# Gathering the experts head by head, with the query projection and the key transposes in the same stage

## The reference

```python
q = einsum('td,de->te', xb, w_q)          # 8 heads x 2 halves x 128
s = einsum('thpd,hpkd->thpk', q, keys)    # 128 scores for each token, head and half
s_top, i_top = lax.top_k(s, 16)
cand = s_top[:, :, 0, :, None] + s_top[:, :, 1, None, :]       # 256 sums for each head
best, sel = lax.top_k(cand, 16)
eidx = (i_top half 0) * 128 + (i_top half 1), taken at sel     # 16 experts for each token and head
gate = softmax(best)
act  = gelu(einsum('td,thkd->thk', xb, u_tab[eidx]))
out  = einsum('thk,thkd->td', gate * act, v_tab[eidx])
```

## Time and profile before

| | us |
|---|---|
| median of 3 runs | 2713.84 (2705.30 to 2722.43) |
| profiled execution | 2712.25 |
| its span | 2710.5 |
| start of the phase `queries` | 1019.67 |
| first gather issued | 1185.48 |
| last gather issued | 2689.80 |

### The profile page before, as it was taken

The page is one execution under the profiler, slowest core; times in us unless marked ns, Lnnn a source line. Parts: engine busy times, 40 slices in busy tenths (PEclk is TensorE's granted clock), DMA queues, the critical chain, the costliest instruction groups (busy, mean ns, idle before and its releaser), DMA issues.

```text
span 2710.5 us, 24179 instructions
## 1 busy us (share of the span) xinstructions
PE 1893.6 (70%) x8692; PEld 1256.1 (46%) x8692; DVE 1364.3 (50%) x2693; ACT 524.8 (19%) x1028; POOL 1161.3 (43%) x1083
## 2 busy tenths in 40 slices
PE   4988696788776878704766676666667575757577
PEld 4987696487646778701323232222223232323232
DVE  2253543511564432386555655656565646564652
ACT  4223121022103242201112111121111121112111
POOL 0010110100011010037677767677767777777774
PEclk9997798699868888957888888787878787878789
DMA  3221111141224304149999999999999999999997
GB/s 113 81 64 47 32 40 44 44 138 42 90 92 149 106 11 124 32 164 325 360 370 367 384 354 365 369 357 375 374 373 350 375 349 385 347 362 362 375 362 282
DMA packets 237486, 632.51 MB, mean 233 GB/s; under 512 B 20655, under 2 KB 97791, under 8 KB 236994
## 3 DMA queue, kind: packets, MB, share of 16 engines
q0 software_dynamic: 149760, 545.33, 53.4%
q1 hardware_dynamic: 87626, 85.92, 10.0%
HBM read 615.46 MB, written 15.80 MB: 233 GB/s over the span
## 4 chain that ended last, share of the span: by engine, by line
issue 56%; PE 2%; DMA 1%; POOL 0%; SPq 0%; DVE 0%; ACT 0%
PE ps L1668 2%; POOL ex_u_row L1621 0%; DMA ex_v_row<-in_peer_v,ex_eidx 0%; DMA ex_gate_s<-again_gate 0%; SPq L1602 0%; DMA again_x<-x_ffn 0%; DVE h_tok L1827 0%; DVE h_tok L1821 0%; ACT ex_junk_a L1705 0%; SPq L1608 0%; ACT ex_ms L1707 0%; SPq L1606 0%; SPq L1605 0%; DVE ex_ms L1826 0%
## 5 line engine op out<-in xcount | busy, mean ns | idle before, releaser
L1668 PE MATMUL ps<-ex_v_row,ex_spread 128*128 128x512 f32 (+1 forms) x2080 | 974.1, 632 | 548.2 <-DMA ex_v_row<-in_peer_v,ex_eidx 495.3
L1668 PEld LDWEIGHTS ps<-ex_v_row,ex_spread 128*128 128x128 f32 (+1 forms) x2080 | 417.2, 202 | 1103.8 <-issue 585.7
L1808 DVE CUSTOM_DVE_ANT_0 ex_u_row<-ex_u_row,x_ffn 128x1024 f32<-128x1024 f32 x512 | 626.8, 1226 | 256.9 <-DMA ex_u_row<-in_peer_u,ex_eidx 224.8
L1621 POOL DMA_INDIRECT ex_u_row<-in_peer_u,ex_eidx x512 | 529.3, 1034 | 328.2 <-DVE ex_gate L1801 168.2
L1621 POOL DMA_INDIRECT ex_v_row<-in_peer_v,ex_eidx x512 | 519.9, 1015 | 270.9 <-issue 158.3
L1699 ACT ACTIVATE ex_spread<-square,ex_coef 128x128 f32<-128x128 f32 (+1 forms) x520 | 204.3, 399 | 1238.5 <-issue 583.8
L1815 DVE TENSOR_TENSOR ex_coef<-ex_coef,ex_gate 128x16 f32<-128x16 f32 x32 | 5.6, 176 | 276.3 <-ACT ex_coef L1692 200.4
L533 PE MATMUL ps<-proj_b_whi,x_lo 128*128 128x256 f32 (+1 forms) x320 | 90.7, 283 | 9.2 <-DVE proj_b_wlo L474 9.2
L582 POOL TENSOR_TENSOR dp_w_lo<-dp_w_raw,dp_w_hi 128x1024 fp32r<-128x1024 f32 x8 | 19.2, 2407 | 167.6 <-ACT dp_w_hi L608 167.6
L326 POOL TENSOR_TENSOR x_ffn<-norm_xn,norm_gains_row 128x1024 f32<-128x1024 f32 (+1 forms) x5 | 14.0, 2810 | 179.1 <-ACT norm_xn L281 179.1
L535 PE MATMUL ps<-proj_b_whi,x_hi 128*128 128x256 f32 (+1 forms) x320 | 90.4, 282 | 0.0
(11 more groups left out here) (392 smaller groups left out, 3504.1 us busy)
## 6 DMA issues: line engine op xcount, KB each, us to landing
ex_u_row<-in_peer_u,ex_eidx POOLq DMA_INDIRECT x512
ex_v_row<-in_peer_v,ex_eidx POOLq DMA_INDIRECT x512
proj_a_raw<-in_w_in SPq DMA_DIRECT2D x7, 1024.0 KB, 4.9
proj_b_raw<-in_w_in SPq DMA_DIRECT2D x7, 1024.0 KB, 5.3
queries_raw<-in_peer_wq SPq DMA_DIRECT2D x7, 1024.0 KB, 5.8
dp_w_raw<-in_w_in SPq DMA_DIRECT2D x8, 512.0 KB, 4.0
S_sample<-in_state_ret SPq DMA_DIRECT2D x1, 4096.0 KB
out_ret_s<-S_sample SPq DMA_DIRECT2D x4, 1024.0 KB, 4.5
```

The costliest lines, as they stand in the source:

```text
L1621: pool.indirect_dma_start(row[n % RING][:, :], None, table, bass.IndirectOffsetOnAxis(ap=where, axis=0)).then_inc(done[n % RING], 16)
L1668: ins = pe.matmul(k.pv[t % 2][0:r, c, :], spread[:, n % RING, 0:r], v_row[n % RING][:, c * 512:(c + 1) * 512], start=(i == 0), stop=(i == ...
L1808: dve.tensor_tensor_reduce(u, u, x, 1.0, 0.0, ALU.mult, ALU.add, coef[:, n:n + 1]).then_inc(dotted, 1)
```

## The change

- The phases `queries` and `turn_keys` are gone. Their work is inside `experts`, for one half head (128 columns, 512 KB of weights) at a time: `upper` on ScalarE, `lower` on VectorE, `queries` on TensorE, and a copy of the product on ScalarE. The keys and the first two blocks of weights are loaded during `norm2`.
- The unit of the retrieval is a head of a tile (32 units and 8 more for the sample tokens). `retrieve(u)` does for one head what the 8 parts did for eight, in fewer instructions or on fewer columns, and reads the scores from PSUM.
- VectorE's order: four `lower`, `retrieve(0)`, two `lower`, `retrieve(1)`, two `lower`, and then for each unit its 16 dots, the retrieval of the unit two ahead, and `weigh`. In units 0, 1 and 2 the last eight `lower` lie between dots. In units 20 to 27 a retrieval of a sample head follows the other one.
- GpSimd issues only gathers of u in units 0, 1 and 2 (`LEAD` = 3). From unit 3 on gathers of u and v take turns one by one, v three units behind; in units 10 and 18 two gathers of v go with each of u, after which v is two units behind, then one.
- `RING` is 7. The residual goes to DRAM during `norm2` (2 MB) and comes back tile by tile to `fin`. The softmax has its exponent and its sum in one ScalarE instruction for each head, with `Exp` and `Gelu` in turns.

The diff, cut to its core; the removed bodies of `turn_keys` and `experts` stand above:

```diff
--- before.py
+++ after.py
...
-GROUP = 16
 PER_ROW = HK * NS // P
-RING = 8
+RING = 7
...
+                for tiles, dst, s in stores:
+                    sp.wait_ge(summed, tiles)
+                    sp.dma_start(dst, s).then_inc(stored, 16)
+                wait(sp, stored, 16 * (len(extra) + len(stores)))
...
+def experts(k, a, o, x_hi, x_lo, x_ffn, h_store, again, early):
...
+    UNITS = TILES * PH
+    SAMPLE = UNITS
...
+    LEAD, BOTH = 3, (10, 18)
+    sums, w = {}, 0
+    for u in range(LEAD, UNITS + 1):
+        sums[u] = range(w, w + 1 + (u in BOTH))
+        w = sums[u].stop
+    summed_in = {w: u for u in sums for w in sums[u]}
+    turns = [0, 1]
+    after = {}
+    for u in range(UNITS):
+        after[u] = [u + 2] * (u + 2 < UNITS) + [SAMPLE + u - 20] * (20 <= u < 20 + PH)
+        turns += after[u]
+    place = {u: j for j, u in enumerate(turns)}
+    known = {u: 2 + sum(len(after[x]) for x in range(u + 1)) for u in range(UNITS)}
...
+        q, keysT = sb("q", [P, HP, T]), sb("keysT", [P, HP, NK])
...
+        x_rep, gain = (w[:, :, :].rearrange("p c n -> p (c n)") for w in w_raw)
+        coef, spread = sb("coef", [P, SLOTS]), sb("spread", [P, RING, P])
+        fin, ms = sb("fin", [P, 2, D]), sb("ms", [P, NT])
...
+        def slots(u):
+            return range(TOPK * u, TOPK * u + (TOPK if u < SAMPLE else PER_ROW))
...
+        def score_bank(j):
+            return k.pb[6 + j % 2][:, 0:2 * NK]
...
+                def fetch(t):
+                    r = ROWS[t]
+                    wait(sp, stored[t % 2], 16 * (t // 2))
+                    sp.dma_start(fin[0:r, t % 2, :], h_store[t * P:t * P + r, :]).then_inc(h_loaded[t % 2], 16)
+                def result(t):
+                    out = o["y_p"][0, t * P:(t + 1) * P, :] if t < TILES else o["y_s"][:, 0, :]
+                    sp.wait_ge(ready, t + 1)
+                    sp.dma_start(out, fin[0:ROWS[t], t % 2, :]).then_inc(stored[t % 2], 16)
+                    if t + 2 < NT:
+                        fetch(t + 2)
...
+                for n in range(2, HP):
+                    sp.wait_ge(split, n - 1)
+                    sp.dma_start(w_raw[n % 2][:, :, :], columns(a["peer_wq"][0], n * P, P)).then_inc(w_loaded[n % 2], 16)
...
+                fetch(0)
+                fetch(1)
+                result(0)
+                result(1)
...
             @block.gpsimd
             def _(pool):
...
+                def up(u, n):
+                    t, h = tile_head(u)
...
+                    wait(pool, dotted, n - RING + 1)
+                    pool.indirect_dma_start(u_row[:, n % RING, :], None, a["peer_u"][0],
+                                            bass.IndirectOffsetOnAxis(ap=where, axis=0)).then_inc(u_loaded[n % RING], 16)
...
+                def down(n):
...
+                    wait(pool, v_done, n - RING + 1)
+                    pool.indirect_dma_start(v_row[:, n % RING, :], None, a["peer_v"][0],
+                                            bass.IndirectOffsetOnAxis(ap=where, axis=0)).then_inc(v_loaded[n % RING], 16)
...
+                for u in range(UNITS + 1):
+                    if u < UNITS:
+                        pool.wait_ge(idx_ready, place[u] + 1)
+                    else:
...
+                    if u == LEAD:
+                        pool.wait_ge(keys_turned, HP // 4)
+                    downs = [n for w in sums.get(u, ()) for n in slots(w)]
+                    for i, n in enumerate(slots(u)):
+                        up(u, n)
+                        for m in downs[i * len(downs) // TOPK:(i + 1) * len(downs) // TOPK]:
+                            down(m)
+                    for m in downs[len(slots(u)) * len(downs) // TOPK:]:
+                        down(m)
+                for m in slots(SAMPLE):
+                    down(m)
...
             @block.tensor
             def _(pe):
...
+                def queries(n):
+                    pe.wait_ge(split, n + 1)
+                    for h in two:
+                        wait(pe, q_done, 2 * n + h - 1)
+                        mm3(pe, k.pb[4 + h][:, 0:HALF], DC, lambda x, c: x[:, c, :], w_hi[n % 2], w_lo[n % 2],
+                            lambda x, c: x[:, c, h * HALF:(h + 1) * HALF], x_hi, x_lo).then_inc(q_mm, 1)
+                def scores(j):
+                    t, h = tile_head(turns[j])
+                    r = ROWS[t]
+                    pe.wait_ge(q_done, 4 * h + 4)
+                    wait(pe, s_free, j - 1)
+                    for p in two:
+                        n = 2 * h + p
+                        ins = pe.matmul(score_bank(j)[0:r, p * NK:(p + 1) * NK], q[:, n, t * P:t * P + r], keysT[:, n, :],
+                                        start=True, stop=True)
+                    ins.then_inc(s_mm, 1)
+                for n in range(HP):
+                    ins = pe.transpose(k.pb[n // 4][:, (n % 4) * P:(n % 4 + 1) * P], keys[:, n, :], k.eye)
+                    if n % 4 == 3:
+                        ins.then_inc(keys_turned, 1)
+                pe.wait_ge(keys_done, HP // 4)
+                for n in range(HP):
+                    queries(n)
+                    if n % 2 and n // 2 < 4:
+                        scores(n // 2)
+                done = 4
+                for u in range(LEAD, UNITS + 2):
+                    for j in range(done, known.get(u, done)):
+                        scores(j)
+                    done = max(done, known.get(u, done))
+                    for w in sums.get(u, (SAMPLE,)):
+                        t, h = tile_head(w)
                         r = ROWS[t]
...
+                        for n in slots(w):
+                            pe.wait_ge(v_loaded[n % RING], 16 * (n // RING + 1))
+                            pe.wait_ge(spread_done, n + 1)
+                            first, last = n % HK == 0, n % HK == (HK if w < SAMPLE else PER_ROW) - 1
+                            for c in two:
+                                ins = pe.matmul(k.pv[t % 2][0:r, c, :], spread[:, n % RING, 0:r],
...
             @block.scalar
             def _(act):
...
+                def upper(n):
+                    if n >= 2:
+                        act.wait_ge(w_loaded[n % 2], 16 * (n // 2))
+                        act.wait_ge(q_mm, 2 * n - 2)
+                    act.activation(w_hi[n % 2][:, :, :], w_raw[n % 2][:, :, :], ACT.Copy).then_inc(rounded, 1)
...
+                upper(0)
+                upper(1)
+                for n in range(HP // 4):
+                    act.wait_ge(keys_turned, n + 1)
+                    act.activation(keysT[:, 4 * n:4 * n + 4, :].rearrange("p a b -> p (a b)"), k.pb[n],
+                                   ACT.Copy).then_inc(keys_done, 1)
+                for n in range(HP):
+                    for h in two:
+                        act.wait_ge(q_mm, 2 * n + h + 1)
+                        act.activation(q[:, n, h * HALF:(h + 1) * HALF], k.pb[4 + h][:, 0:HALF], ACT.Copy).then_inc(q_done, 1)
+                    if n + 2 < HP:
+                        upper(n + 2)
...
+                for u in range(LEAD):
+                    weight(u)
+                    gelu(u)
+                for u in range(LEAD, UNITS + 1):
+                    if u == UNITS - 2:
+                        for h in range(PH):
+                            weight(SAMPLE + h)
+                    for t in range(TILES - 1):
+                        if u == summed_in[t * PH + PH - 1] + 2:
+                            root(t)
+                    for w in sums[u]:
+                        spreads(w)
+                    if u < UNITS:
+                        weight(u)
+                    gelu(u)
+                spreads(SAMPLE)
...
             def _(dve):
                 own = Own(dve, own_s)
...
+                def lower(n):
+                    dve.wait_ge(rounded, n + 1)
+                    wait(dve, q_mm, 2 * n - 2)
+                    dve.tensor_tensor(w_lo[n % 2][:, :, :], w_raw[n % 2][:, :, :], w_hi[n % 2][:, :, :].bitcast(F32),
+                                      ALU.subtract).then_inc(split, 1)
+                def retrieve(u):
+                    j = place[u]
+                    t, h = tile_head(u)
...
+                    ps = score_bank(j)[0:r, :].rearrange("p (n c) -> p n c", n=2)
...
+                    dve.wait_ge(s_mm, j + 1)
+                    for p in two:
+                        ins = dve.max(top[0:r, p, eights[0]], ps[:, p, :])
+                    own.fence(ins)
+                    for p in two:
+                        dve.max_index(top_i[0:r, p, eights[0]], top[0:r, p, eights[0]], ps[:, p, :])
+                    for p in two:
+                        ins = dve.match_replace(rest[0:r, p, :], top[0:r, p, eights[0]], ps[:, p, :], LOWEST)
+                    fence(dve, ins, s_free, j + 1)
...
+                    dve.tensor_scalar(pick[0:r, 0, :], sel[0:r, :], 4, None, ALU.logical_shift_right)
```

(53 more changed lines are left out.)

342 lines of the change are left out of this document (103 added, 239 removed).

## The result

The changed kernel took 2764.11 us (median of 4 runs, 2756.78 to 2773.96) where the kernel before took 2713.33 on the same chip: a ratio of 1.0188, 95% interval 1.0137 to 1.024. So it is slower on this chip; whether by 2% the interval leaves open. The profiled execution took 2757.49 us, its span 2755.7. The forecast was 2640, range 2565 to 2705.

A forecast was written before the change was run, and what follows sets the result against it. The last 1500 us were taken as bound by moving rows, the work before the gathers as serial, with GpSimd becoming the bound; 1156 + 1426 + 5 + 28 + 3 + 20.7 - 2 = 2637 us of span, so 2640, range 2565 to 2705.

The forecast's parts named there:

- the length of `retrieve` beside the gathers: One head's retrieval on VectorE: 8.8 us, bounds 6.6 and 11, hidden behind some 10 gathers or 12.4 us.
- Head, 1156 for gather 48: Work ahead of gather 48: first gather 134 us earlier, gather 48 at 1156 instead of 1263.93, so 108 us left.
- Start of v, +5: First v gathers: `retrieve(4)` waits some 5 us for head 4's scores, delaying `weigh` and the first v slot: +5 us.
- `norm2`: Phase ahead of the new stage: 2 us added at its end for storing 2 MB late and loading 2 MB early.
- Turns of one, price 0: u and v gathers alternating: GpSimd 45.8 us a unit against 46.0, so pace unchanged; bounds -55 and +41 us.
- Double retrieval, +28: Units 20 to 27: VectorE away 17.6 us, 3.5 us lost in each of eight units, +28 us; bounds 0 and 70.
- longer gathers beside lone dots: GpSimd gathers beside dots standing alone: 0.48 us extra on the mean; 11 such dots a unit.
- Tail, 20.7 - 2: From last gather issue to span end: 20.7 us as before, less 2 for fewer unpaired v gathers, 16 instead of 24.
- The sum, 2637 of span: Whole kernel: 1156 + 1426 + 5 + 28 + 3 + 20.7 - 2 = 2637 us of span, giving a 2640 us forecast.
- C of the forecast: Rival, 5%: gather and dot exclude each other for their whole length, 1.555 us a gather, 2755 us.
- A: Rival, 15%: the DMA engines fill, 1.383 us a gather, 2560 us; needs a dot to cost GpSimd under 0.3 us.
- D: Rival, 3%: TensorE stays at half the clock, 520 slots at 3.4 us from 1172 on end at 2940.

The follow-up runs named there:

- A: Chip of the result: kernel before 2713.3 us, changed kernel 2764.1 us, ratio 1.0188.
- F: Another chip: changed kernel as it is 2745.0 us, ratio 1.0129; changed kernel with each retrieval in four parts between dots 2618.2 us, 0.968.
- C: Another chip: changed kernel 2614.2 us (0.9689); before 2706.9; before with rings of 7 2757.3 (1.0236); change with sample retrieval mid-unit 2588.1 (0.9595).
- D: Another chip, VectorE steps added in retrievals: change 2716.9 us (1.0087), before 2697.4 (1.0011), sample retrieval mid-unit 2642.1 (0.9803), four parts 2576.9 (0.9565).
- the first trace: Trace of the changed kernel in the first result, nothing else edited: median 2764.11 us, ratio 1.0188 to the kernel before.
- E: Another chip, steps added on VectorE and ScalarE: change 2818.9 us (1.0413), before 2729.4 (1.0077), four parts 2616.6 (0.9658); retrieval in two parts, nothing added, 2610.7 (0.9641).
- B: Another chip: change with blocks of 16 2671.5 us (0.99), sample retrieval mid-unit 2591.1 (0.9607), four parts 2592.2 (0.9594); before with turns of one 2725.3 (1.0092).
- the version in four parts: Changed kernel with every retrieval from unit 3 on cut in four parts with dots between (double ones in eight): 2592.2 us, 0.9594; with 167 added VectorE steps 0.9565.

## Why the prediction was wrong

**What failed is one step: the length of `retrieve` beside the gathers, and with it that a single one is hidden.** I took its 8.8 us from tile 0, whose retrieval ran at DMA share 0.00, set the bounds at 6.6 and 11, and used it unchanged for the 36 retrievals beside full DMA queues ("VectorE is away for 8.8 us behind each unit ... so this is hidden"). Undisturbed it is 8.51 to 8.54 (8.34 for sample tokens), also at a DMA share of 1.0, so the sum of steps was good. On chips A and F 25 and 23 of the 36 are over 10 us, up to 18.9. What they were set against was right: "some 10 gathers or 12.4 us" of cover, measured mostly 9 or 10 gathers and 12.1 to 13.8 us. The upper bound of 11 lay under that cover and 18.9 lies over it, so GpSimd stops. The evidence stood in the trace of before ("13.2 <-issue"): a stage that hides idle time of VectorE shows it without paying for it. Runs on A, C, D and F carry this: with the late steps 1.019 and 1.013, without them 0.969, put in by hand 1.009. Four fifths of the difference are shown so; the rest is open.

**Head, 1156 for gather 48:** right: 1149.3 on A, 1151.1 on C, 1148.7 on F. **Start of v, +5:** `retrieve(4)` waited 8.5 us on A, 4.3 on C and 14.7 on F, forecast 5. **`norm2`:** nothing against it.

**Turns of one, price 0:** right as a sum, for reasons partly missed. On C, double retrievals taken apart, the pace is 1.426 against 1.432 of before. I forecast longer gathers beside lone dots (in the changed kernel there 1.10 us for u and 1.13 for v on the mean, forecast 1.0 and 1.2), and that GpSimd becomes the bound; in fact its DMA share in 1200 to 2000 is 0.99 at 376 GB/s, so both limits meet. What I had left out is `RING` 7 for 8: 60 us in a kernel with blocks of 16, and with the turns no sign of it. That the total came out on C owes something to this luck.

**Double retrieval, +28:** right, 26 us on C. On A these units lost more, through late steps.

**Tail, 20.7 - 2:** 19.0, both in the first trace and on C.

**The sum, 2637 of span:** 2624.9 on C (gather 48 5 us earlier, the pace 1.468 for 1.475), 2755.7 on A. **Rivals:** none named what happened. C of the forecast was the only one that ended slower, and not by its mechanism: no gather had to wait for a whole dot, which would make 0.94 + 1.23 = 2.17 us; the longest in the changed kernel, on A and C alike, is 1.99, and the pace on C was 1.468 where C of the forecast had 1.555. The Trainium skill (SBUF — State Buffer, Who interferes with whom) calls the port pair that VectorE and GpSimd share an exclusive lock. For gathers beside dots these traces show a delay, and no lock for the whole instruction. The versions without double retrieval come near A (2588 against 2560; DMA share 0.99 in 1200 to 2000 and 0.97 in 2040 to 2500 on C). D did not come: in 1200 to 2000 the granted clock was 0.94 on A and 0.98 on C, in 2040 to 2500 it was 0.82 and 0.85. The slots at 1.2 GHz on A follow waits, as behind 1432.07 above.

**What stays open.** What makes steps late was not shown. They appear on A, E and F, where the kernel before runs in 2708 to 2713, and not on B, C and D, where it runs in 2697. They were seen only beside gathers at a DMA share near 1.0, VectorE's in runs of short steps. One idea is that instructions arrive late from memory; the page lists queues of kind "instruction", with 60 loads of 16 KB on the larger:

```profile
q8 instruction: 60, 0.98, 0.1%
q14 instruction: 49, 0.40, 0.0%
```

The Trainium skill (Runtime: NRT & Kernel Launch, Instruction fetch mechanics) says that each sequencer fetches its instructions over a DMA queue of its own, in 16 KiB blocks, and that this is mostly hidden. The size agrees with the rows above. That late loads make the steps late the trace does not bear out. Of the 86 late steps of VectorE on A only 6 have a transfer of either queue in flight in the idle time before them, and with these idle times shifted by multiples of 7 us it is 5.7 on the mean; of 45 late spreads it is 4, and 5.4 when shifted. Past 1150 us a load of the larger queue took 1.04 us on A and 1.06 on C. When a load was asked for the trace does not show. Of the last fifth of the difference, ScalarE's share is unsettled. The transfers can have 17 us at most: the gathers' packets took 53.1% of 2755.7 us on A and 55.1% of 2624.9 on C, 1463 and 1446 us.

## What to carry to other kernels

Price a sequence of small dependent instructions from a place where it stands beside the same work as where you move it to, and read the idle time between its steps even where it costs nothing: a block of other work may be hiding it. When one engine serves a ring that another engine fills, compare its longest absence, not its mean load, with what the ring covers, and cut the absence into parts between the services: here parts of 2 us gave 0.957 to 0.968 on four chips (B, D, E, F), where one piece gave 0.969 to 1.019 on three (A, C, F). And measure on more than one chip before a verdict of 2%.

## What had not been expected of the hardware

- The same program differs by 5.7% between chips (2614 and 2764 us), while another that computes the same differs by 0.6% (2697 and 2713).
- Steps of VectorE that depend on nothing but the step before start up to 6.1 us late (on F), and a spread on ScalarE up to 11.6 us (on A), on some chips, at a DMA share near 1.0; on others the same steps show none of it at the same share.
- More work on VectorE cost nothing: 167 added steps of 0.69 us in the version in four parts gave 0.9565 against 0.9594 without them, on two chips, with overlapping intervals.
- A gather's issue beside a lone dot is longer than alone (up to 1.99 us for 0.94), and still the pace held, since the DMA engines were at 0.99.
